# Rotary turns and head norms on pairs of tiles, the context's jobs emitted earlier, a longer pitch in the context's norms

## The chip, the core and the metric

The kernel runs on one core of a Trainium2 chip. The metric is the device time of one execution in microseconds; three runs of the kernel before gave 2795.01, 2799.68 and 2804.26 us, median 2799.68. Engines are PE (TensorE), DVE (VectorE), ACT (ScalarE), POOL (GpSimd) and SP, which issues the weight loads.

## What is computed

A sequence of 256 tokens with 1024 features goes through two blocks. The first has two layers: a pooling and gating mixer with a SwiGLU feed-forward, and a mixer of sparse attention (8 heads) and retention (4 heads) with another. The second has two layers, each feed-forward, attention, feed-forward, modulated by rows of an adaptive norm. It carries a context of 256 tokens beside the sequence:

```python
for i in range(2):
    m, mc = adaln(c, ada_w[i], ada_b[i]), adaln(c_ctx, ada_w[i], ada_b[i])
    h  = half_ffn(h,  m,  0, ...)              # the sequence
    hc = half_ffn(hc, mc, 0, ...)              # the context
    u, uc = modulated_norm(h, g[2], m, 3), modulated_norm(hc, g[2], mc, 3)
    y, yc = diff_attention(u, uc) if i == 0 else gqa_axial(u, uc)
    h = half_ffn(gated_residual(h, y, ...), m, 6, ...)
    if i == 0: hc = half_ffn(gated_residual(hc, yc, ...), mc, 6, ...)
```

Queries and keys get a rotary turn, `x * cos + swap(x) * sin`, where `swap` is a product with a fixed 128x128 matrix. Heads are normalised by their root mean square over 128 features (a head norm): after retention (4 tiles), after differential attention (8 tiles, sequence and context) and on queries and keys of the last attention (10 tiles of the sequence, 2 of the context).

## The kernel before

Activations lie with features on the partitions: a tile is 128 features by 256 tokens (`T`), so a 1024-wide activation is 8 tiles. Every dense product is done to full precision with three fp32r matmuls: a weight block of 128x2048 is loaded to `raw`, ACT copies it to `whi` (L208), DVE subtracts to `wlo` in two halves (L215, L228), and PE takes hi*hi, hi*lo and lo*hi (L249), 24 matmuls for each half block, 48 for a block.

Three generators produce work. `x_sequence` is the sequence (lane X), `c_sequence` the context (lane C), `modulation` the adaptive norm's rows (lane A). They yield `("D",)` before a block, `("d",)` between its two halves, and `("L", us)` where the next step should come no sooner than `us` of the planner's clock. X drives: at each of its D and d, `pace` (L1063) may take one or two steps of the others and adds 2.9 to the clock for a half block; at each of its L, `fill(us)` (L1049) advances the clock by 2.2 times `us` and takes dense steps of C (or A) as long as they are due. A step of C whose L is not over is not taken, and then `fill` leaves PE to X. Before each attention X calls `want("kv0")` or `want("kv1")`, which runs C to the end of its keys and values, whatever its L. The order thus made is the program order of every engine, and each engine's queue is served in that order.

- `turn` (L694) turns one tile: a 256-wide fp32 matmul with the swap matrix into a side bank (L698), then on DVE a product with sin from PSUM into `TMPX` (L700), a product with cos in place (L701) and a sum (L703). 41 tiles are turned: 15 in the sparse mixer, 16 in differential attention, 10 in the last. Where two or three banks are used in turn, the matmul of the third waits for L700 of the first.
- `tile_norm` (L721) works on one tile at a time: Square on ACT (L730), two column sums on PE (L736) with an L of 0.6 at every second tile, Sqrt (L741), reciprocal and scale (L744, L746); then per tile a diagonal (two 128-wide `tensor_scalar`, L753), its spreading with a ones matmul (L760), and the scaling (L766), with an L of 0.8 at every second tile; with `keep`, also a hi and lo part (L772, L778). X has two buffers for squares and diagonals, C one. 32 tiles are normalised.
- `norm` (L564) is the norm over 1024 features, with the residual. Its loop writes tile k of the next input in three steps over DVE, POOL and ACT (L607, L613, L656, L661, L670); in lane C it yields an L of 2.5 at every second turn, six in all. C goes through it five times.
- `after` (L279) holds back the job that empties a C bank (the gate's L428, the up product's L441, the down product's L492 with `put_out`, or an evacuation): it is emitted when C registers its next job, or by `settle` (L287) at the end of a part. Lane X emits its own at once.

## Time and profile before

| | |
|---|---|
| median of three runs | 2799.68 us |
| profiled execution | 2801.2 us, span 2799.5 us |
| PE busy | 2588.8 us (92%) |
| DVE busy | 1694.4 us (61%) |
| ACT busy | 1251.0 us (45%) |
| POOL busy | 132.2 us (5%) |
| mean granted TensorE clock | 0.959 |

The span runs from the first to the last instruction; the execution has 1.7 us around it. Busy time is the union of an engine's instructions. A wait is counted for the engine that sat idle, under the instruction that it waited with and the one that released it.

### The profile page before, as it was taken

The page shows a single profiled execution, that of the slowest core. Times are in us where ns is not written, and L with a number is a line of the kernel's source. Part 1 is how long each engine was busy: PE and PEld are TensorE (multiplying, and loading weights), DVE is VectorE, ACT ScalarE, POOL GpSimd, SP SyncE. Part 2 cuts the span into 40 slices and gives each one's busy share as a digit, 9 for nine tenths or more (in the row PEclk, how much of TensorE's full clock was granted, in tenths as well). Part 3 has the DMA queues.
Part 4 walks back from the last instruction along what each step waited for, and adds up shares of the span by engine and source line. Part 5 has one row for each costly group of instructions (what it writes and reads, how often), then busy time and mean ns, then how long its engine had stood idle before and what let it go on. Part 6 is the DMA issues. An engine that isn't in the chain of part 4 may idle for free.

```text
span 2799.5 us, 48887 instructions
## 1 busy us (share of the span) xinstructions
PE 2588.8 (92%) x20706; PEld 2461.9 (88%) x20706; DVE 1694.4 (61%) x2807; ACT 1251.0 (45%) x1698; POOL 132.2 (5%) x174
## 2 busy tenths in 40 slices
PE   6799998999998999999898999999999998987998
PEld 5699988888888899999797989999999998966998
DVE  5665564456666556466666757676566566555654
ACT  4533342344444344454444544454454454334443
POOL 0000000000012000000020000020000010000000
PEclk9899998899999999999899999999999999988999
DMA  6556655523445665544342334554545544444453
GB/s 231 196 187 248 242 181 193 211 104 108 166 163 199 222 247 185 192 153 155 103 144 83 121 124 168 179 174 165 182 168 181 177 166 144 165 147 170 151 178 124
DMA packets 68616, 475.80 MB, mean 170 GB/s; under 512 B 7984, under 2 KB 8496, under 8 KB 14768
## 3 DMA queue, kind: packets, MB, share of 16 engines
q1 hardware_dynamic: 66240, 468.74, 47.3%
q10 hardware_dynamic: 2160, 3.93, 0.5%
q8 instruction: 165, 2.70, 0.4%
q14 instruction: 51, 0.42, 0.0%
HBM read 471.60 MB, written 1.05 MB: 169 GB/s over the span
## 4 chain that ended last, share of the span: by engine, by line
PE 71%; DVE 11%; issue 7%; ACT 6%; DMA 4%; POOL 1%; ACTq 0%; DVEq 0%; POOLq 0%
PE bank L249 61%; ACT whi L208 4%; DVE wlo L228 2%; DMA raw<-w_main 2%; PE bank L994 2%; DVE wlo L215 1%; DMA raw<-w_down 1%; PE bank L876 1%; PE bank L814 1%; PE bank L1323 1%; PE bank L736 1%; DVE ARX L656 1%; DVE HNC_lo L670 1%; PE bank L760 1%; PE bank L864 1%
## 5 line engine op out<-in xcount | busy, mean ns | idle before, releaser
L249 PE MATMUL bank<-HNX_hi,whi 128*128 128x256 f32 x2968 | 866.4, 293 | 54.8 <-DVE wlo L228 30.9
L249 PE MATMUL bank<-HNX_hi,wlo 128*128 128x256 f32 x2968 | 851.8, 288 | 0.0
L208 ACT ACTIVATE whi<-raw 128x2048 fp32r<-128x2048 f32 (+1 forms) x378 | 705.6, 1867 | 306.2 <-PE bank L249 138.8
L249 PE MATMUL bank<-HNX_lo,whi 128*128 128x256 f32 x2968 | 838.5, 288 | 0.0
L215 DVE TENSOR_TENSOR wlo<-raw,whi 128x1024 fp32r<-128x1024 f32 (+1 forms) x378 | 454.3, 1202 | 605.5 <-ACT whi L208 604.8
L249 PEld LDWEIGHTS bank<-HNX_hi,whi 128*128 128x128 f32 x2968 | 585.9, 197 | 75.1 <-issue 46.1
L249 PEld LDWEIGHTS bank<-HNX_hi,wlo 128*128 128x128 f32 x2968 | 585.7, 197 | 0.0
L249 PEld LDWEIGHTS bank<-HNX_lo,whi 128*128 128x128 f32 x2968 | 577.8, 197 | 0.5
L228 DVE TENSOR_TENSOR wlo<-raw,whi 128x1024 fp32r<-128x1024 f32 (+1 forms) x378 | 453.1, 1199 | 0.0
L249 PE MATMUL bank<-HNC_hi,whi 128*128 128x256 f32 x1344 | 395.9, 295 | 20.2 <-DVE tmpc L428 9.5
L249 PE MATMUL bank<-HNC_lo,whi 128*128 128x256 f32 x1344 | 386.6, 288 | 0.0
L249 PE MATMUL bank<-HNC_hi,wlo 128*128 128x256 f32 x1344 | 386.4, 287 | 0.0
L249 PE MATMUL bank<-GX_hi,whi 128*128 128x256 f32 x1056 | 302.8, 287 | 3.0 <-DVE wlo L228 2.9
L249 PE MATMUL bank<-GX_lo,whi 128*128 128x256 f32 x1056 | 299.1, 283 | 0.0
L249 PE MATMUL bank<-GX_hi,wlo 128*128 128x256 f32 x1056 | 299.0, 283 | 0.0
L249 PEld LDWEIGHTS bank<-HNC_hi,whi 128*128 128x128 f32 x1344 | 264.4, 197 | 29.1 <-DVE tmpc L428 10.5
L249 PEld LDWEIGHTS bank<-HNC_lo,whi 128*128 128x128 f32 x1344 | 264.5, 197 | 0.5
L249 PEld LDWEIGHTS bank<-HNC_hi,wlo 128*128 128x128 f32 x1344 | 264.2, 197 | 0.0
L249 PEld LDWEIGHTS bank<-GX_hi,whi 128*128 128x128 f32 x1056 | 202.9, 192 | 8.9 <-DVE wlo L228 4.4
L249 PEld LDWEIGHTS bank<-GX_lo,whi 128*128 128x128 f32 x1056 | 202.9, 192 | 0.1
L249 PEld LDWEIGHTS bank<-GX_hi,wlo 128*128 128x128 f32 x1056 | 202.8, 192 | 0.0
L445 ACT ACTIVATE GX_hi<-tmpx 128x512 fp32r<-128x512 f32 x66 | 41.7, 632 | 262.5 <-DVE tmpx L441 262.5
(320 smaller groups left out, 3134.8 us busy)
## 6 DMA issues: line engine op xcount, KB each, us to landing
raw<-w_main SPq DMA_DIRECT2D x270, 1024.0 KB, 4.8
raw<-w_ada SPq DMA_DIRECT2D x72, 1024.0 KB, 4.8
raw<-w_down SPq DMA_DIRECT2D x72, 1024.0 KB, 4.9
raw<-w_down SPq DMA_DIRECT2D x36, 768.0 KB, 4.2
raw<-w_cmp SPq DMA_DIRECT2D x4, 1024.0 KB, 4.7
HX<-x_in SPq DMA_DIRECT2D x2, 512.0 KB, 6.2
HC<-ctx_in ACTq DMA_DIRECT2D x1, 1024.0 KB, 7.3
out<-HX SPq DMA_DIRECT2D x4, 256.0 KB, 2.1
```

What stands on the lines that cost most here:

```text
L208: NS.activation(WHI[q % HIS][:, 0:size], RAW[m % SLOTS][:, 0:size], ACT.Copy).then_inc(sems["w_hi"], 1)
L215: NV.tensor_tensor(WLO[m % SLOTS][:, 0:half], RAW[m % SLOTS][:, 0:half], WHI[q % HIS][:, 0:half].bitcast(fp32), SUB)
L228: NV.tensor_tensor(WLO[m % SLOTS][:, half:size], RAW[m % SLOTS][:, half:size], WHI[q % HIS][:, half:size].bitcast(fp32), SUB).then_inc(sem ...
L249: return NT.matmul(dst, (WHI[ordinal[n] % HIS], WLO[n % SLOTS])[w][:, k * 2 * P + col:k * 2 * P + col + P], x[xp][:, kx, :], start=start, ...
L445: NS.activation(g[0], S.TMP[p % 2][:, :], ACT.Copy).then_inc(hi.sem, 1)
L656: NV.scalar_tensor_tensor(S.Y[:, k, :], S.H[:, k, :], gain(k), S.wide_h[:, 0:T], MUL, MUL).then_inc(no.sem, 1)
L670: NV.scalar_tensor_tensor(S.HN[1][:, k, :], S.Y[:, k, :], shift(k), S.HN[0][:, k, :].bitcast(fp32), ADD, SUB)\
L736: mm = NT.matmul(sums[:, 2 * j + c:2 * j + c + 1], b[:, c * P:(c + 1) * P], ones[:, 0:1], start=True, stop=True)
L760: NT.matmul(bank[:, 0:T], ones, b[:, :], start=True, stop=True).then_inc(sp_.sem, 1)
L814: mm = NT.matmul(bank[:, c0 + c * T:c0 + (c + 1) * T], q[pr, :], k[pr, :], start=True, stop=True)
L864: mm = NT.transpose(turn_bank[:, c * P:(c + 1) * P], PB[w % 3][:, 0, c * P:(c + 1) * P], ident)
L994: mm = NT.matmul(bank[32 * g:32 * g + 32, 0:T], CCOL[:, k, 6 - 2 * r:38 - 2 * r], RAW[n % SLOTS][:, k * T:(k + 1) * T], start=r == 0 and k ...
```

## The change

- `turn` takes a pair of tiles (one stays alone): one 512-wide matmul and three 512-wide DVE operations. 21 calls in place of 41.
- `tile_norm` takes pairs: one 512-wide Square, four column sums, one diagonal as a `tensor_tensor` of 512 with two broadcast inputs, one 512-wide spreading matmul, one scaling (two after retention, whose gains differ). An L of 0.8 stands ahead of every pair's sums and one of 1.0 ahead of every pair's spreading. The product with 1.0 is left out. X's buffers are `TMPX[1]` and the joined squares buffer, C's is `TMPC[1]`. 16 pairs in place of 32 tiles.
- `catch_up` at the head of `pace` and `fill` emits C's held job as soon as a further block of any lane has been taken.
- The L in the loop of C's `norm` is 6.0 in place of 2.5.

```diff
-        SQX, SQC = [sb(f"sqx{s}", [P, T])[:, :] for s in range(2)], [sb("sqc", [P, T])[:, :]]
+        SQ2, SQC = sb("sqx", [P, 2 * T]), [sb("sqc", [P, T])[:, :]]
+        SQX = [SQ2[:, s * T:(s + 1) * T] for s in range(2)]
...
                 last, jobs[S.tag] = jobs.get(S.tag), job
+                behind[0] = len(taken)
                 if last:
                     last()
+
+            def catch_up():
+
+                if "c" in jobs and len(taken) > behind[0]:
+                    settle(C)
...
                     if t == "c" and j % 2 == 0:
-                        yield ("L", 2.5)
+                        yield ("L", 6.0)
                     if t == "x" and j == 4:
                         yield ("L", 4.0)
...
-            def turn(tile, rot, cos, sin, bank, j, *ready):
+            def turn(tiles, rot, cos, sin, bank, j, *ready):
 
                 turned, part, straight, done_ = up("pe_step"), up("dve_step"), up("dve_step"), up("dve_step")
+                n = tiles.shape[1]
+                swapped, kept = (x[:, 0:n * T].rearrange("p (a b) -> p a b", a=n) for x in (bank, TMPX[j % 2]))
                 if on(pe, free.get(bank.name), *ready):
-                    NT.matmul(bank[:, 0:T], rot, tile, start=True, stop=True).then_inc(turned.sem, 1)
+                    NT.matmul(swapped, rot, tiles, start=True, stop=True).then_inc(turned.sem, 1)
                 if on(dve, turned):
-                    NV.tensor_tensor(TMPX[j % 2][:, 0:T], bank[:, 0:T], sin, MUL).then_inc(part.sem, 1)
-                    NV.tensor_tensor(tile, tile, cos, MUL).then_inc(straight.sem, 1)
+                    NV.tensor_tensor(kept, swapped, sin.unsqueeze(1).to_broadcast([P, n, T]), MUL).then_inc(part.sem, 1)
+                    NV.tensor_tensor(tiles, tiles, cos.unsqueeze(1).to_broadcast([P, n, T]), MUL).then_inc(straight.sem, 1)
                     dve.wait_ge(*straight)
-                    NV.tensor_tensor(tile, tile, TMPX[j % 2][:, 0:T], ADD).then_inc(done_.sem, 1)
+                    NV.tensor_tensor(tiles, tiles, kept, ADD).then_inc(done_.sem, 1)
                 free[bank.name] = part
                 return done_
...
 
-            def tile_norm(S, items, gain, factor, ready, eps, sums, banks, keep=False):
-
-
-                n, last = len(items), {}
-                buf = S.TMP[0][:, 0:2 * n]
-                for j, src in enumerate(items):
+            def tile_norm(S, pairs, gain, factor, ready, eps, sums, banks, keep=False, alike=True):
+
+
+                n, last = len(pairs), {}
+                buf = S.TMP[0][:, 0:4 * n]
+                wide = [S.TMP[1][:, :]] if S.lag else [S.TMP[1][:, :], SQ2[:, :]]
+                for j, src in enumerate(pairs):
                     sq = up("act_step")
-                    b = S.SQ[j % len(S.SQ)]
-                    if on(act, last.get(j - len(S.SQ)), *ready):
-                        NS.activation(b[:, :], src, ACT.Square).then_inc(sq.sem, 1)
-                    if j % 2:
-                        yield ("L", 0.6)
+                    b = wide[j % len(wide)]
+                    if on(act, last.get(j - len(wide)), *ready):
+                        NS.activation(b.rearrange("p (a q) -> p a q", a=2), src, ACT.Square).then_inc(sq.sem, 1)
+                    yield ("L", 0.8)
                     total = up("pe_step")
                     if on(pe, sq, free.get(sums.name) if j == 0 else None):
-                        for c in range(2):
-                            mm = NT.matmul(sums[:, 2 * j + c:2 * j + c + 1], b[:, c * P:(c + 1) * P], ones[:, 0:1], start=True, stop=True)
+                        for c in range(4):
+                            mm = NT.matmul(sums[:, 4 * j + c:4 * j + c + 1], b[:, c * P:(c + 1) * P], ones[:, 0:1], start=True, stop=True)
                         mm.then_inc(total.sem, 1)
                     last[j] = total
-                root, inv, fac = up("act_step"), up("dve_step"), up("dve_step")
+                root, inv = up("act_step"), up("dve_step")
+                fac = inv if factor is None else up("dve_step")
                 if on(act, total):
-                    NS.activation(buf, sums[:, 0:2 * n], ACT.Sqrt, bias=eps, scale=1.0 / P).then_inc(root.sem, 1)
+                    NS.activation(buf, sums[:, 0:4 * n], ACT.Sqrt, bias=eps, scale=1.0 / P).then_inc(root.sem, 1)
                 free[sums.name] = root
                 if on(dve, root):
                     NV.reciprocal(buf, buf).then_inc(inv.sem, 1)
                     dve.wait_ge(*inv)
-                    NV.tensor_scalar(buf, buf, 1.0 if factor is None else factor, None, MUL).then_inc(fac.sem, 1)
+                    if factor is not None:
+                        NV.tensor_scalar(buf, buf, factor, None, MUL).then_inc(fac.sem, 1)
                 spreads, his, los, marks = {}, [], [], []
 
                 def diagonal(j):
-                    b, bank, diag = S.SQ[j % len(S.SQ)], banks[j % len(banks)], up("dve_step")
-                    if on(dve, fac, spreads.get(j - len(S.SQ)), total):
-                        for c in range(2):
-                            op = NV.tensor_scalar(b[:, c * P:(c + 1) * P], ident, buf[:, 2 * j + c:2 * j + c + 1], None, MUL)
-                        op.then_inc(diag.sem, 1)
+                    b, diag = wide[j % len(wide)], up("dve_step")
+                    if on(dve, fac, spreads.get(j - len(wide)), total):
+                        NV.tensor_tensor(b.rearrange("p (c q) -> p c q", c=4), ident.unsqueeze(1).to_broadcast([P, 4, P]),
+                                         buf[:, 4 * j:4 * j + 4].unsqueeze(2).to_broadcast([P, 4, P]), MUL).then_inc(diag.sem, 1)
                     return diag
 
                 def spread(j, diag):
-                    b, bank, sp_ = S.SQ[j % len(S.SQ)], banks[j % len(banks)], up("pe_step")
+                    bank, sp_ = banks[j % len(banks)], up("pe_step")
                     if on(pe, diag, free.get(bank.name)):
-                        NT.matmul(bank[:, 0:T], ones, b[:, :], start=True, stop=True).then_inc(sp_.sem, 1)
+                        NT.matmul(bank[:, :], ones, wide[j % len(wide)], start=True, stop=True).then_inc(sp_.sem, 1)
                     spreads[j] = sp_
 
-                def scale_tile(j):
+                def scale_pair(j):
                     bank, sc = banks[j % len(banks)], up("dve_step")
                     if on(dve, spreads[j]):
-                        NV.scalar_tensor_tensor(items[j], items[j], gain(j), bank[:, 0:T], MUL, MUL).then_inc(sc.sem, 1)
+                        if alike:
+                            NV.scalar_tensor_tensor(pairs[j], pairs[j], gain(2 * j), bank[:, :].rearrange("p (a q) -> p a q", a=2), MUL, MUL)\
+                                .then_inc(sc.sem, 1)
+                        else:
+                            for m in range(2):
+                                op = NV.scalar_tensor_tensor(pairs[j][:, m, :], pairs[j][:, m, :], gain(2 * j + m), bank[:, m * T:(m + 1) * T], MUL, MUL)
+                            op.then_inc(sc.sem, 1)
                     free[bank.name] = sc
                     marks.append(sc)
                     if keep:
                         hi = up(f"{S.tag}_hn_hi")
                         if on(act, sc):
-                            NS.activation(S.HN[0][:, j, :], items[j], ACT.Copy).then_inc(hi.sem, 1)
+                            NS.activation(S.HN[0][:, 2 * j:2 * j + 2, :], pairs[j], ACT.Copy).then_inc(hi.sem, 1)
                         his.append(hi)
 
                 def keep_low(j):
                     lo = up(f"{S.tag}_hn_lo")
                     if on(dve, his[j]):
-                        NV.tensor_tensor(S.HN[1][:, j, :], items[j], S.HN[0][:, j, :].bitcast(fp32), SUB).then_inc(lo.sem, 1)
+                        NV.tensor_tensor(S.HN[1][:, 2 * j:2 * j + 2, :], pairs[j], S.HN[0][:, 2 * j:2 * j + 2, :].bitcast(fp32), SUB).then_inc(lo.sem, 1)
...
                     los.append(lo)
                 diag = diagonal(0)
                 for j in range(n + 1):
                     if j < n:
-                        if j % 2 == 0:
-                            yield ("L", 0.8)
+                        yield ("L", 1.0)
                         spread(j, diag)
-                        if len(S.SQ) > 1 and j + 1 < n:
+                        if len(wide) > 1 and j + 1 < n:
                             diag = diagonal(j + 1)
-                        scale_tile(j)
-                        if len(S.SQ) == 1 and j + 1 < n:
+                        scale_pair(j)
+                        if len(wide) == 1 and j + 1 < n:
                             diag = diagonal(j + 1)
...
             def fill(us, passing=0.0):
 
+                catch_up()
                 if ahead["c"] == "W":
...
             def pace(kind):
 
+                catch_up()
                 if ahead["c"] == "W":
                     step("c")
...
-                for j, t in enumerate((4, 6, 8)):
-                    roped = turn(Z[:, t, :], *ROT, side[j], j, z_kv[-1])
+                for j, t in enumerate((4, 8)):
+                    roped = turn(Z[:, t:t + 3 - 2 * j:2, :], *ROT, side[j], j, z_kv[-1])
...
+                todo = [(z0[-1], t) for t in (8, 10)]
                 for b, at in [(7, 14), (8, 16), (9, 18), (10, 20), (11, 22), (0, 0), (1, 2), (2, 4), (3, 6)]:
-                    for j, (m, t) in enumerate(todo[:2]):
-                        roped = turn(Z[:, t, :], *ROT, side[j], j, m)
-                    todo = todo[2:]
+                    for m, t in todo[:1]:
+                        roped = turn(Z[:, t:t + 2, :], *ROT, side[t // 2 % 2], t // 2, m)
+                    todo = todo[1:]
...
-                nrm = yield from tile_norm(X, [RO[:, h, :] for h in range(4)], lambda h: vec("gn_g", h, 1), None, [cen, g1], vec("eps5"), BANK[4], BANK[2:4])
+                nrm = yield from tile_norm(X, [RO[:, h:h + 2, :] for h in (0, 2)], lambda h: vec("gn_g", h, 1), None, [cen, g1], vec("eps5"), BANK[4], BANK[2:4], alike=False)
...
-                normed = [0, 1, *range(4, 12)]
-                nqk = yield from tile_norm(X, [Z[:, t, :] for t in normed], lambda j: vec("k_norm" if j < 2 else "q_norm"), None, [z[-1], vt],
+                normed = [0, 4, 6, 8, 10]
+                nqk = yield from tile_norm(X, [Z[:, t:t + 2, :] for t in normed], lambda j: vec("k_norm" if j < 2 else "q_norm"), None, [z[-1], vt],
...
-                kn = yield from tile_norm(C, [KC[:, g, :] for g in range(2)], lambda j: vec("k_norm"), None, [zk[-1]], vec("eps6"), BANK[7], BANK[6:7])
+                kn = yield from tile_norm(C, [KC[:, 0:2, :]], lambda j: vec("k_norm"), None, [zk[-1]], vec("eps6"), BANK[7], BANK[6:7])
```

The other callers of `turn` and `tile_norm` change in the same way.

## Rows read from the trace of the kernel before

**Rows 1.** The page: busy time, share and instructions of each engine; engines' shares of the chain.
```profile
PE 2588.8 (92%) x20706; PEld 2461.9 (88%) x20706; DVE 1694.4 (61%) x2807; ACT 1251.0 (45%) x1698; POOL 132.2 (5%) x174
...
PE 71%; DVE 11%; issue 7%; ACT 6%; DMA 4%; POOL 1%; ACTq 0%; DVEq 0%; POOLq 0%
```

**Rows 2.** PE's waits, whole span: in total us, times, longest us.
```profile
PE bank L249 <- DVE wlo L228: 35.5, 17, 7.7
...
PE bank L760 <- DVE sqc L753: 9.7, 5, 3.0
PE bank L249 <- DVE tmpc L428: 9.5, 5, 3.2
...
PE bank L760 <- DVE sqx L753: 7.8, 8, 1.5
...
PE bank L249 <- DVE tmpc L441: 5.4, 4, 2.8
...
PE bank L736 <- ACT sqc L730: 4.5, 5, 1.5
...
PE bank L698 <- DVE tmpx L700: 4.1, 9, 0.7
...
PE bank L736 <- ACT sqx L730: 3.3, 3, 1.2
PE bank L249 <- DVE ARC L492: 2.4, 1, 2.4
```

**Rows 3.** Groups by line: busy us, mean ns of one, idle before, releaser.
```profile
L428 DVE SCALAR_TENSOR_TENSOR tmpx<-tmpx,bank 128x512 f32<-128x512 f32 x66 | 45.3, 686 | 53.1 <-ACT tmpx L426 52.9
...
L700 DVE TENSOR_TENSOR tmpx<-bank,ARX 128x256 f32<-128x256 f32 x41 | 17.2, 420 | 24.5 <-PE bank L698 24.5
...
L766 DVE SCALAR_TENSOR_TENSOR ARX<-ARX,VEC,bank 128x256 f32<-128x256 f32 x22 | 10.5, 478 | 3.1 <-PE bank L760 3.0
...
L1312 DVE TENSOR_TENSOR ARX<-ARX 64x480 f32<-64x480 f32 x4 | 3.9, 968 | 4.2 <-PE bank L1323 4.1
...
L1517 PE MATMUL bank<-ARX,VEC 128*128 128x512 f32 x4 | 2.0, 590 | 0.0
```

**Rows 4.** The chain in order of time, 1372 to 1406 us: start, us, what.
```profile
1377.42 2.98 PE bank L249 x24
...
1383.67 0.40 DVE sqc L753 x2
...
1384.12 1.22 PE bank L760 x2
1385.34 3.83 PE bank L249 x24
```

**Rows 5.** Timeline, 1378 and 908 us on: start, us, instruction, idle before and releaser.
```profile
1380.12 0.74 PEld L698 LDWEIGHTS bank<-ARX,VEC 128*128 128x128 f32 x4
...
910.86 1.89 ACT L208 ACTIVATE whi<-raw 128x2048 fp32r<-128x2048 f32 x1
...
915.50 1.22 DVE L228 TENSOR_TENSOR wlo<-raw,whi 128x1024 fp32r<-128x1024 f32 x1
...
916.87 0.55 PE L249 MATMUL bank<-HNX_hi,whi 128*128 128x256 f32 x1 [6.74 <-DVE wlo L228]
```

**Rows 6.** Busy time in four stretches: us, then PE, PEld, DVE, ACT, POOL, clock, DMA share, GB/s.
```profile
136.00:172.00 36.00, 31.16 (x216) 29.79 (x217) 25.75 (x54) 14.42 (x20) 5.75 (x8) 0.81 0.35 123
...
1487.00:1511.00 24.00, 12.54 (x68) 9.91 (x69) 19.56 (x47) 13.17 (x29) 5.75 (x8) 0.79 0.05 18
1511.00:1618.00 107.00, 106.27 (x866) 99.84 (x864) 74.10 (x130) 58.13 (x105) 0.00 (x0) 1.00 0.34 119
...
2449.00:2485.00 36.00, 27.05 (x111) 18.12 (x111) 20.17 (x62) 6.70 (x14) 0.00 (x0) 0.76 0.15 49
```

**Rows 7.** Instructions of L661 and L760: duration ns min/median/max, first and last start.
```profile
L661 ACT ACTIVATE HNC_hi<-ARC,MOD x40: 494/508/513, 117.8 to 2334.1; 128x256 fp32r<-128x256 f32 x40
...
L760 PE MATMUL bank<-sqc,VEC x20: 377/379/797, 1381.1 to 2371.6; 128*128 128x256 f32 x20
```

More of the change, by code:

```diff
@@ L163, in program @@
             NV, NS, NT, NG = nc.vector, nc.scalar, nc.tensor, nc.gpsimd
-            taken, split_at, opened, jobs = [], [0, 0, 0], [None], {}
+            taken, split_at, opened, jobs, behind = [], [0, 0, 0], [None], {}, [0]
             free, passed, gains_known = {}, set(), {}
@@ L1337, in x_sequence @@
                 blk = blocks_of(1, hid)
-                for t in range(4):
-                    roped = turn(Z[:, t, :], *ROT, side[t % 2], t, z_q[-1])
+                for t in range(0, 4, 2):
+                    roped = turn(Z[:, t:t + 2, :], *ROT, side[t // 2], t // 2, z_q[-1])
                 z_v = yield from linear(X, "od_in", [(9, 18), (10, 20)], Z)
@@ L1356, in x_sequence @@
                 z_rk = yield from linear(X, "od_in", [(7, 14)], Z)
-                for j, t in enumerate(range(10, 14)):
-                    roped = turn(Z[:, t, :], *ROT, side[j % 2], j, z_rq[-1])
+                for j, t in enumerate((10, 12)):
+                    roped = turn(Z[:, t:t + 2, :], *ROT, side[j], j, z_rq[-1])
                 turned, th = up("pe_step"), up("act_step")
@@ L1375, in x_sequence @@
                 z_rg = yield from linear(X, "od_in", [(11, 22)], Z)
-                for j, t in enumerate(range(14, 18)):
-                    roped = turn(Z[:, t, :], *ROT, side[j % 2], j, z_rk[-1])
+                for j, t in enumerate((14, 16)):
+                    roped = turn(Z[:, t:t + 2, :], *ROT, side[j], j, z_rk[-1])
                 z_rg = yield from linear(X, "od_in", [(12, 24)], Z)
@@ L1555, in x_sequence @@
                     dve.wait_ge(*in_tab)
-                todo = [(z0[-1], t) for t in range(8, 12)]
+                todo = [(z0[-1], t) for t in (8, 10)]
                 for b, at in [(7, 14), (8, 16), (9, 18), (10, 20), (11, 22), (0, 0), (1, 2), (2, 4), (3, 6)]:
-                    for j, (m, t) in enumerate(todo[:2]):
-                        roped = turn(Z[:, t, :], *ROT, side[j], j, m)
-                    todo = todo[2:]
+                    for m, t in todo[:1]:
+                        roped = turn(Z[:, t:t + 2, :], *ROT, side[t // 2 % 2], t // 2, m)
+                    todo = todo[1:]
                     z = yield from linear(X, "da_in", [(b, at)], Z)
                     if b == 7:
-                        todo += [(z1[-1], t) for t in (12, 13)] + [(z[-1], t) for t in (14, 15)]
+                        todo += [(z1[-1], 12), (z[-1], 14)]
                     elif b < 4:
-                        todo += [(z[-1], t) for t in (at, at + 1)]
+                        todo.append((z[-1], at))
                     if b == 11:
@@ L1568, in x_sequence @@
                 vt = None
-                for j, (m, t) in enumerate(todo):
-                    roped = turn(Z[:, t, :], *ROT, side[j % 2], j, m)
+                for m, t in todo:
+                    roped = turn(Z[:, t:t + 2, :], *ROT, side[t // 2 % 2], t // 2, m)
                 vt = by_token([Z[:, 16 + h, c * P:(c + 1) * P] for c in range(2) for h in range(8)], VTX, side, z_v)
@@ L1580, in x_sequence @@
                 passed.add("x_da")
-                x = yield from tile_norm(X, [YX[:, h, :] for h in range(8)], lambda h: vec("subln"), 1.0 - LAMBDA_INIT, [o], vec("eps6"), BANK[4], BANK[2:4], True)
+                x = yield from tile_norm(X, [YX[:, h:h + 2, :] for h in range(0, 8, 2)], lambda h: vec("subln"), 1.0 - LAMBDA_INIT, [o], vec("eps6"), BANK[4], BANK[2:4], True)
                 free["x", "gain"] = need(0, 5)
@@ L1612, in x_sequence @@
                 for j, t in enumerate(normed):
-                    roped = turn(Z[:, t, :], *ROT, side[j % 3], j, nqk)
+                    roped = turn(Z[:, t:t + 2, :], *ROT, side[j % 3], j, nqk)
                 want("kv1")
@@ L1685, in c_sequence @@
                 o = yield from attend_context(units, 0.125, PB, PT, LAM, [vt, l5, zq[-1]])
-                x = yield from tile_norm(C, [YC[:, h, :] for h in range(8)], lambda h: vec("subln"), 1.0 - LAMBDA_INIT, [o], vec("eps6"), BANK[7], BANK[6:7], True)
+                x = yield from tile_norm(C, [YC[:, h:h + 2, :] for h in range(0, 8, 2)], lambda h: vec("subln"), 1.0 - LAMBDA_INIT, [o], vec("eps6"), BANK[7], BANK[6:7], True)
                 free["c", "gain"] = yield from await_rows(0, 5)
```

## The prediction

> **What bounds the kernel now.** First the page: PE is busy 92% of the span, and 71% of the chain that ended last is PE, 11% DVE [rows 1]. So the time is PE's work plus the 210.7 us in which it idles (2799.5 less 2588.8), and an edit pays as far as it shortens one of the two. DVE at 61% is no bound on average; locally it is. The second view is the list of PE's waits [rows 2]: the largest, 35.5 us, is for a block's `wlo`, that is for DVE (and ACT before it) being late with a weight block. Then come the head norms: 9.7 and 7.8 us for diagonals (C's and X's), 4.5 and 3.3 for squares. Waits for a C bank that its job hasn't emptied are 9.5 (L428), 5.4 (L441) and 2.4 us (L492), and turns wait 4.1 us for one another's bank. The third view is the busy time by stretch [rows 6], which tells where C's blocks cover X's gaps, and what is left bare.
>
> **Head norms and turns, PE.** Both spreads of two tiles stand in one step, so the second waits until DVE has scaled the first and made the next diagonal. At 1384.12 this ends in two passes of 1.22 us, and the 24 matmuls behind it take 3.83 us where the ones ahead took 2.98 [rows 4]: the clock had fallen. In the change each spread has its own L, so a half block of 2.98 us stands between two. That covers 0.69 us of diagonal (the 686 ns of a 512-wide PSUM operation stands for it [rows 3]) and 0.75 of scaling (478 ns plus 256 columns at the slope of L700 to L428, 420 to 686, so 744). Of the 17.5 us of waits for diagonals I take off 14.5; 3 stay, the first diagonal of each norm and the last attention, where no C block is left. Of 7.8 for squares I take off 4.8: the sums that stood right behind their Square now have an L between, but the first of each norm may still come late. Of 4.1 for side banks 3.6 go: no group in the sparse mixer has a third turn any more. The waits of turns for L392's evacuation stay, since a pair waits for the same one. Warm clock regained: 0.85 us behind the wait in rows 4, three to four such places, 3 us.
>
> Matmul width: the second 256 columns of a 512-wide matmul cost 590-379 = 211 ns a pass (L1517 against the warm L760 [rows 3, 7]), two passes. Two tiles apart take four passes, paced by four weight loads in 0.74 us (at 1380.12 [rows 5]), so 0.19 each; a pair takes two of 0.21 and its loads behind another's passes, 0.55. So 0.2 us a pair, of 20 turn pairs and 16 norm pairs less the ten in the last attention where DVE bounds: 26 x 0.2 = 5.2 us.
>
> The last attention's head norm and turns lie bare: 2449 to 2485, PE at clock 0.76 [rows 6]. The turns there run at DVE's pace, three operations; each pair saves three fixed parts of 420-266 = 154 ns, 5 x 0.46 = 2.3 us, less 0.7 for a longer first matmul and its last pair. Spreads take two scalings and four diagonals (0.2 us each, 0.40 for two [rows 4]) in a pair of tiles, 1.7 us with the waits 2.2; in pairs 1.3 to 1.5: 5 x 0.8 = 4 us, of which about 2 are already in the waits. Sum 3.5. The column sums stay as many, and they set the pace of the squares.
>
> Sum of this part: 14.5+4.8+3.6+3+5.2+3.5 = 34.6; I take 33, since part of the freed time meets the next wait, `wlo`. From below: if DVE only hands the wait on, half, 17. From above 40.
>
> The price that the trace doesn't show is the diagonal with an input that stands still along the row (one scalar for 128 columns). Bounds: 0.69 us as for any 512-wide operation, and 0.97 for 480 elements with a still input and a strided one (L1312 [rows 3]). I take 0.69, since only one of L1312's inputs is like it and the strides there are long; at 1.0 it would be 16 x 0.3 = 5 us of DVE, behind half blocks mostly, 2 us of the end.
>
> The skill speaks against this edit: the Trainium skill, VectorE: DVE Perf Modes, "The perf-mode tier table (the rule you actually need)", gives fp32 `tensor_scalar` two elements a cycle and `tensor_tensor` one. By it the pair's 512 columns would stream 0.27 us longer, 4.3 us over 16 pairs. The rows have the four old operations at 0.8 us together, so the saved fixed parts pay for it, and no term of the sum changes.
>
> **C's jobs emitted earlier.** C's bank waits sum to 17.3 us (9.5+5.4+2.4) [rows 2], 10 places. A job held from a block long past, with X's blocks since, is emitted with `catch_up` behind the next block; then the bank is free long before C returns. Where two C blocks follow each other within one `fill`, nothing changes. I take 9 of 17.3. The last four down products of C's feed-forward emit three `put_out` in a row, and the longest wait for `wlo` (7.7 us) is of that kind; spread by one block each, it loses 3 us. What is moved is ACT's and DVE's work alone (no DMA, SP's queue isn't passed; POOL gets its sums a block sooner). The job now stands in front of X's second `wlo` half at places; it waits for a C block that PE has ended or is ending, so it holds up DVE for a microsecond or so, and the half is needed two blocks later: 0 to +5 us, taken as 0. Sum -12, from -20 to +5.
>
> **Longer pitch in C's norms.** Five norms (40 hi tiles, 117.8 to 2334.1 [rows 7]), six steps each: 6 x 3.5 = 21 planner units more, about 21 us at 2.9 a half block of 2.98. A step puts some 2.6 us on DVE, an estimate: 19.56 us busy in 1487 to 1511 [rows 6], less 3 units at about 3.1, over four steps. A block's `wlo` takes 2 x 1.22 [rows 5] beside it. At one step a half block DVE has more work than PE: at 910.86 `whi` starts late behind C's tiles on ACT, `wlo` ends at 916.7, and PE has idled 6.74 us [rows 5]. With the pitch of 6.0 a step falls on two to three half blocks, and DVE fits. Gain: 8 us at 916 with its cold clock, and of the same kind 4, 3 and 2 at three others, an estimate from the rest of the 35.5 us: -17.
>
> Against it stands the cover. X's own `fill`s can only take dense steps of C when C isn't in an L. (a) 136 to 172: C's first norm ends just ahead of X's norm, and two C blocks fill it. Now C is still in its own norm; the two blocks (11.9 us) come later, in X's full stretches, and X's gap saves perhaps 6 of them: +6. (b) 1487 to 1511: C's norm of six steps lies over the first units of X's attention, PE 12.5 of 24 us [rows 6]. A filled unit takes 107/16, so 6.7 us at most, and PE is full then [rows 6]. At 6.0 a step takes two `fill`s (3.0+4.0 planner units), so the six last about four units longer. Each bare unit takes 4.2 to 5.9 us with no C block of 5.96 in it, which costs 3 to 4: 4 x 3.5 = +14 with the relief of what stalls there now. (c) C's end comes later, so its last norm meets X's norm: +2. Sum -17+22 = +5, from -15 to +25.
>
> **Sum.** -33-12+5 = -40 on the profiled execution's 2801.2 us gives 2761. The order of the blocks changes from the first norm on, and new waits of the weight split can't be read from rows of another order: an allowance of +4 for them, one longish wait of rows 2. Forecast 2765 us; the profiled execution is 1.5 us above the median of the runs shown, so nothing is to be shifted.
>
> **Rivals.**
> 1. The waits are handed on: DVE is as busy as before near the norms, and what goes from rows 2 at L760 and L736 comes back at `wlo`. For it: 35.5 us are waits for DVE already, and C's head norm stands where DVE is fullest. Against it: pairs also take work off DVE (turns 41 x 3 x 0.42 = 52 us against 21 x 3 x 0.69 = 43). Then -17-5+5: 2784 us.
> 2. The cover lost is nothing: C's later blocks fill X's norm at the last attention, as bare as 2449 to 2485. Then (a) to (c) cancel: -33-12-17 gives 2739 us.
> 3. The pitch costs more than all gives: C ends too late. Its last head norm is at 2371.6 [rows 7], and X wants kv1 at about 2484 [rows 6]: 112 us. Three norms at +21 make 63, and the four blocks left over in the attention come at one for one of X's, 4 x 11.9 = 48: 111. From there on `want` runs C's rest bare: norm chain, two blocks, a head norm, 35 us. Against it: the planner's clock runs 2.2 times in X's `fill`s, which carries C's L steps along. It decides from the point where C ends later than X's turns. Then -33-12+5, +35 for the bare rest and +20 as the waits are handed on as in rival 1: 2816 us, slower.
> 4. It does nothing that can be told: gains of 20 and losses of 20, 2800 us.
>
> **Chances.** The measurement tells about 0.3%, 8.4 us. Forecast (2752 to 2778) 0.50; rival 1 (2779 to 2792) 0.20; rival 2 (2735 to 2751) 0.14; no difference 0.09; rival 3 0.07. Faster 0.84, same 0.09, slower 0.07. Range 2738 to 2794: it leaves out rival 3, rival 4 and the far end of rival 2.
>
> **What would show it.** Right: waits at L760 and L736 under 7 us together (25.3 now); L698 for L700 near nothing; C's waits for L428 and L441 at half; no 6.7 us gap in C's second norm; the bare stretch around 2449 shorter by 3 to 4; PE less busy by 5; C's hi tiles of the third norm spread over some 40 us. Wrong: `wlo` waits above 35 us; a diagonal above 0.8 us; C's kv1 head norm behind X's turns.

## The result and the profile after

The kernel after takes 2736.55 us (median of 4 runs, 2734.23 to 2740.13), the kernel before, measured beside it, 2799.51: ratio 0.9776, 95% interval 0.9756 to 0.9796. That is 63 us less, where 35 were forecast; 2736.55 is 1.5 us below the lower end of the range. The direction was right, the size was not.

The page after, the two lines that answer to [rows 1]:

```profile
PE 2561.5 (94%) x20634; PEld 2428.9 (89%) x20634; DVE 1677.2 (61%) x2674; ACT 1241.1 (45%) x1668; POOL 127.7 (5%) x174
...
PE 76%; DVE 11%; ACT 5%; issue 3%; DMA 3%; POOL 1%; ACTq 0%; DVEq 0%; POOLq 0%
```

The span fell from 2799.5 to 2733.6 us. PE's idle time fell from 210.7 to 172.1, by 38.6 us, and its busy time by 27.3. The prediction counted mostly waits, and took only some 8 us off PE's own work (5.2 for the width, 3 for the clock).

PE's waits after, whole span (in total us, times, longest), against [rows 2]:

```profile
PE bank L250 <- DVE wlo L229: 25.5, 18, 6.0
PE bank L250 <- ACT HNX_hi L668: 14.9, 12, 5.3
PE bank L879 <- DVE ARX L843: 12.9, 7, 3.1
PE bank L250 <- ACT HNX_hi L666: 12.6, 5, 5.6
...
PE bank L829 <- DVE KC L777: 4.9, 1, 4.9
...
PE bank L250 <- DVE tmpc L435: 2.9, 1, 2.9
...
PE bank L745 <- ACT tmpx L740: 2.3, 2, 1.5
...
PE bank L250 <- DVE tmpc L448: 2.1, 2, 1.1
...
PE bank L770 <- DVE tmpc L763: 0.7, 1, 0.7
...
PE bank L707 <- DVE tmpx L709: 0.2, 1, 0.2
```

(L760 is L770 now, L736 L745, L698 L707, L428 L435, L441 L448.) Diagonals cost 0.7 us in place of 17.5, squares 2.5 in place of 7.8, the side banks 0.2 in place of 4.1, C's banks (L435, L448) 5.0 in place of 14.9, `wlo` 25.5 in place of 35.5. What grew stands in the second to fourth line: the waits for the hi tiles of X's own norms (L668 from 4.0 us, L666 from 8.5), and those for L843, the DVE step that combines the two softmax parts in X's differential attention (from 0.8). There PE waited before for ACT's exponentials instead, 9.7 us in two waits against 2.3 in one now.

The groups by line with shapes apart, for the price that was not to be seen before (busy us, mean ns of one, idle before):

```profile
L763 DVE TENSOR_TENSOR tmpx<-VEC,tmpx 128x512 f32<-128x512 f32 x6 | 4.1, 688 | 0.2
...
L777 DVE SCALAR_TENSOR_TENSOR ARX<-ARX,VEC,bank 128x512 f32<-128x512 f32 x9 | 6.7, 744 | 8.7 <-PE bank L770 8.7
...
L709 DVE TENSOR_TENSOR tmpx<-bank,ARX 128x512 f32<-128x512 f32 x20 | 13.8, 688 | 23.6 <-PE bank L707 23.6
...
L712 DVE TENSOR_TENSOR ARX<-ARX,tmpx 128x512 f32<-128x512 f32 x20 | 13.9, 693 | 0.7
```

The broadcast diagonal takes 0.69 us, the value taken and not the 0.97 of L1312 in [rows 3]; the scaling 744 ns is what was worked out. The four `tensor_scalar` of a pair before (L753) kept DVE busy for 0.95 us, 15.2 us in all over the 16 pairs; the 16 new diagonals take 10.9.

### The profile page after: what moved, and what is told of

Same layout as the page of the kernel before. It is cut to its first block, busy times and chain, and to the rows that moved or that the text cites. A ratio compares the mean times of both kernels' runs of the same rounds, so it can differ in the third digit from the quotient of the medians.

```text
span 2733.6 us, 48496 instructions
## 1 busy us (share of the span) xinstructions
PE 2561.5 (94%) x20634; PEld 2428.9 (89%) x20634; DVE 1677.2 (61%) x2674; ACT 1241.1 (45%) x1668; POOL 127.7 (5%) x174
## 4 chain that ended last, share of the span: by engine, by line
PE 76%; DVE 11%; ACT 5%; issue 3%; DMA 3%; POOL 1%; ACTq 0%; DVEq 0%; POOLq 0%
PE bank L250 66%; ACT whi L209 3%; DMA raw<-w_main 2%; DVE wlo L229 2%; PE bank L1009 2%; DVE wlo L216 1%; DMA raw<-w_down 1%; PE bank L891 1%; PE bank L829 1%; DVE ARX L663 1%; PE bank L1340 1%; DVE tmpx L614 1%; PE bank L707 1%; DVE HNX_lo L677 1%; PE bank L879 1%
## 5 line engine op out<-in xcount | busy, mean ns | idle before, releaser
L250 PE MATMUL bank<-HNX_hi,whi 128*128 128x256 f32 x2968 | 865.8, 293 | 58.9 <-DVE wlo L229 21.1
L250 PEld LDWEIGHTS bank<-HNC_hi,whi 128*128 128x128 f32 x1344 | 259.2, 193 | 17.3 <-issue 6.9
```

The costliest lines, as they stand in the source:

```text
L250: return NT.matmul(dst, (WHI[ordinal[n] % HIS], WLO[n % SLOTS])[w][:, k * 2 * P + col:k * 2 * P + col + P], x[xp][:, kx, :], start=start, ...
```

## The experiments

Ratios are to the kernel before on the same chip, with a 95% interval; a difference in us is taken from the ratio or the medians, which agree within 3 us. "Idle" is the span less PE's busy time of the profiled execution (210.7 us before).

**The three parts alone.** First the pairs without the two others.

```diff
-                        yield ("L", 6.0)
+                        yield ("L", 2.5)
...
             def fill(us, passing=0.0):
 
-                catch_up()
...
             def pace(kind):
 
-                catch_up()
```

> The change's pairs alone (turns and head norms), C's jobs held as before, pitch 2.5. The changed kernel gained 63 us where 35 were forecast, so a term was too small. Theory 1 (the pairs' term was right, 33 us, and another was wrong): 2767 us, ratio 0.988. Theory 2 (the pairs carry the surplus as well, since every DVE operation saved comes back as PE time): 2745 us or less, ratio 0.980. In both the waits at the spreading matmul and the sums fall from 25.3 to under 7 us.

Measured 2763.53 us, 0.9871 (0.9857 to 0.9886): -36. Idle fell by 22.9, busy by 14.5:

```profile
PE 2574.3 (93%) x20634; PEld 2441.6 (88%) x20634; DVE 1680.8 (61%) x2674; ACT 1246.5 (45%) x1674; POOL 132.4 (5%) x174
```

The waits for `wlo` stay (33.6 us), so nothing was handed on to them; C's banks (L435, L448, L499) came to 21.1 us in place of 17.3, so some 4 us were handed on there.

The earlier emission alone, on the kernel before:

```diff
             def fill(us, passing=0.0):
 
+                catch_up()
...
             def pace(kind):
 
+                catch_up()
```

> The early emission of C's jobs alone, single tiles, pitch 2.5. Theory 1 (as forecast): 12 us, ratio 0.996. Theory 2 (its term was the small one: bank waits 17.3 us go nearly whole, and the wait for the weight split that three jobs in a row cause goes as well, with the clock): 25 us or more, ratio 0.991. A rival: it stands in front of X's second half of the weight split and gives nothing, ratio 1.0.

Measured 2781.36 us, 0.9938 (0.9923 to 0.9953): -18. Its page and its waits:

```profile
PE 2582.5 (93%) x20706; PEld 2455.3 (88%) x20706; DVE 1690.2 (61%) x2807; ACT 1253.2 (45%) x1698; POOL 129.6 (5%) x174
```

```profile
PE bank L249 <- DVE wlo L228: 38.5, 21, 6.7
...
PE bank L249 <- DVE tmpc L434: 6.0, 2, 3.0
...
PE bank L249 <- DVE ARC L498: 1.3, 1, 1.3
...
PE bank L249 <- DVE tmpc L447: 1.0, 1, 1.0
```

C's bank waits are 8.3 us in place of 17.3: the 9 that were taken. `wlo` gave nothing (38.5 for 35.5, though its longest went from 7.7 to 6.7). Idle fell by 13.7 and busy by 6.3, with the same 20,706 matmuls.

The longer pitch alone:

```diff
-                        yield ("L", 2.5)
+                        yield ("L", 6.0)
```

> The pitch of 6.0 in the loop of C's norm alone. Theory 1 (as forecast): 17 us gained where the steps crowd DVE and ACT, 22 lost for blocks of C that no longer fill X's gaps, together 5 us slower, ratio 1.002. Theory 2 (the loss was overstated, since fill runs the planner's clock 2.2 times as fast and the norm in the attention is hardly longer): 10 to 17 us faster, ratio 0.995.

Measured 2786.63 us, 0.9962 (0.9947 to 0.9976): -11, where +5 was forecast. Here the prediction failed.

Emission and pitch together:

> Early emission and pitch 6.0, single tiles. If the parts add up, its gain is the sum of the two alone. If they work on the same stall (DVE and ACT crowded where C's feed-forward ends and its norm begins), it is less than the sum by some 5 us; theory 1 has 7 us (ratio 0.9975), theory 2 has 35 (0.9875).

Measured 2773.04 us, 0.9907 (0.989 to 0.9924): -26, against 18+11 = 29. The three parts add within the noise: 36+18+11 = 65, against 63. No cost of a new order of blocks, beyond what each part carries, is to be seen.

**The pitch, norm by norm.** A counter makes the pitch 6.0 in chosen norms of C only; the numbers in the list change from kernel to kernel.

```diff
+                nth[0] += t == "c"
...
-                        yield ("L", 2.5)
+                        yield ("L", 6.0 if nth[0] in (1,) else 2.5)
```

> The kernel before, with the pitch of 6.0 in C's first norm alone (the other four keep 2.5). The prediction's term (a): C's first norm ends after X's, the two C blocks that filled X's norm (11.9 us) stand in X's full stretches instead: +6 us, 2806. Rival (the cover lost is nothing, because C's half blocks of its own norm lie in X's gap instead, or C's blocks find another gap): within 2 us of 2799.5. The longer pitch as a whole measured about 11 to 13 us of gain; if that came from norm 1, 2790.

Measured 2790.54 us, 0.9983 (0.9973 to 0.9992): -5, not +6. X's norm lay as bare as forecast. The windows of it (us, then PE, PEld, DVE, ACT, POOL, clock, DMA share, GB/s):

```profile
133.00:163.00 30.00, 17.16 (x97) 13.94 (x98) 21.97 (x52) 13.03 (x20) 5.72 (x8) 0.66 0.30 114
```

PE works 17 of 30 us at a clock of 0.66. X's first gate comes at 162.9 us in place of 170.1: 7.2 us earlier with two C blocks (11.9 us) fewer, so 4.7 were lost, near the 6 of term (a).

Where do the two blocks come instead? X's six feed-forwards cut the span into seven stretches that hold the same X work in every run (lane A's differs by up to 24 matmuls), and C's blocks in each can be counted. Of the matmuls that read the hi tiles of C's norms (two of the three products of a block), the third stretch, from X's second feed-forward to its third, has in the kernel before, and then with 6.0 in the first norm (us; PE; clock; DMA share, GB/s):

```profile
806.20:1092.70 286.50, 30.34 (x160) 0.98 0.59 212
```

```profile
788.70:1084.70 296.00, 42.28 (x224) 0.97 0.59 212
```

64 more are 96 matmuls with the low parts, that is the two blocks (its down products, which read other tiles, are as many in both). They stand in X's full stretch, as the prediction said, and lengthen it by some 9.6 us. So term (a) as told comes to 9.6-7.2, +2.4. What makes the run faster lies between: the second stretch, from the first to the second feed-forward, is 10.3 us shorter with the same 28 blocks of C. Its idle time is 27.2 us in place of 34.6. One wait that is gone is the fourth of PE's from 290 to 806 us before,

```profile
PE bank L1008 <- ACT rows L1003: 4.3, 1, 4.3
```

and waits for C's banks are 8.1 in place of 10.9. No block was spent on it that the kernel before didn't spend there too; C only runs two blocks further behind. Why that order idles less was not tried.

> The kernel before, with the pitch of 6.0 in C's third norm alone. The prediction's term (b): four more units of X's differential attention stay bare at 3.5 us each, +14 us, 2813. Rival: the attention's bare units are paid back, since a C block that isn't spent beside the first units covers later ones, so the term is nothing: 2797 to 2801. A third way: the norm doesn't spread over the attention's units at all (the planner's clock runs 2.2 times there, so that a step of 6.0 takes not much more than one call), and the relief of DVE makes it faster by 3 to 5, 2795.

Measured 2802.79 us, 1.0017 (1.0008 to 1.0027): +5, a third of the +14. Two waits grew over the whole span, `wlo` (35.5 before) and the combining step of X's attention (0.8 before, while its exponentials went from 9.7 to 2.3):

```profile
PE bank L249 <- DVE wlo L228: 41.9, 18, 7.7
PE bank L865 <- DVE ARX L829: 14.4, 7, 3.9
```

> The kernel before, with the pitch of 6.0 in C's second, fourth and fifth norm. The prediction's gain of 17 us (8 at 916, the rest at the others): 2783 to 2785. If the gain is DVE's relief but smaller, as the whole pitch measured, 2788 to 2790. Theory that the pitch gains nothing by itself but shifts the order: no telling, 2795 to 2803.

Measured 2781.53 us, 0.995 (0.9934 to 0.9967): -14, against the 17 forecast. The wait of 6.74 us at 916 in [rows 5] is gone; from 880 to 940 us PE waits 2.3 us in all for `wlo`.

```profile
PE bank L249 <- DVE wlo L228: 28.4, 18, 7.7
...
PE bank L249 <- DVE tmpc L428: 6.4, 4, 3.1
```

The three add: -5+5-14 = -14, against -11 together. The stretches of the profiled executions, in us with C's blocks in brackets, show where it comes from. "Before" is the kernel before, then 6.0 in the named norms alone; then three versions in the changed order, which are the subject of the next part. Stretches that a run leaves alone differ by up to some 4 us between executions.

| stretch, up to the first gate of X's | before | 1st | 3rd | 2nd, 4th, 5th | changed order, 2.5 in all | after | after, 2.5 in 3rd |
|---|---|---|---|---|---|---|---|
| 1st feed-forward | 170.1 (2) | 162.9 (0) | 172.0 (2) | 168.4 (2) | 173.7 (2) | 163.3 (0) | 161.0 (0) |
| 2nd | 636.2 (28) | 625.8 (28) | 635.9 (28) | 636.1 (28) | 619.5 (28) | 610.5 (28) | 613.5 (28) |
| 3rd | 286.4 (8) | 296.0 (10) | 288.3 (8) | 281.2 (8) | 282.7 (8) | 290.0 (10) | 290.1 (10) |
| 4th, behind differential attention | 654.2 (36) | 651.3 (36) | 630.3 (31) | 652.6 (36) | 632.5 (36) | 607.9 (31) | 631.1 (36) |
| 5th | 364.6 (27) | 364.6 (27) | 360.8 (26) | 322.2 (21) | 361.7 (27) | 325.7 (21) | 320.0 (21) |
| 6th, behind the last attention | 494.2 (16) | 494.1 (16) | 520.2 (22) | 522.9 (22) | 484.1 (16) | 542.5 (27) | 514.7 (22) |

The rest behind the 6th gate takes 194 us in all of them. A C block's own work is 5.96 us. With 6.0 in the second, fourth and fifth norm, the second norm gives 5 us (286.4 to 281.2, with the same blocks). The larger part is six blocks that leave the fifth stretch, which gets 42.4 us shorter, and come in the sixth, which gets only 28.7 longer: their work is 35.8 us, so 7 were gained where they left and 7 where they came. With 6.0 in the third norm, five blocks fewer make X's attention stretch 23.9 us shorter (29.8 would be no loss), and six more the sixth 26.0 longer. By the profiled executions these stretches together lose nothing; the medians of ten runs say +5.

**The pitch in the changed order.** The kernel after with 2.5 in the first and third norm, then in the third alone (the diff), then with 9.0 in the four others, with 2.5 in all five, and once more as it is.

```diff
-                        yield ("L", 6.0)
+                        yield ("L", 2.5 if nth[0] in (3,) else 6.0)
```

> The kernel after, with the pitch of 2.5 again in C's first and third norm. If the prediction's terms (a) and (b) hold in this order too, it beats the kernel after by up to 20 us, 2717 to 2730. If the longer pitch pays or costs nothing at these two, it is as fast as the kernel after or slower: 2735 to 2745.

Measured 2733.73 us, 0.9778 (0.9764 to 0.9793): as the kernel after.

> The kernel after, with the pitch of 2.5 again in C's third norm alone. In the order of before the longer pitch cost 5 us in the third norm and gained 5 in the first. If both are so here too: 2731 to 2732, and 2 us less than with 2.5 in the first and third. If the order matters more than the pitch, anything from 2728 to 2742.

Measured 2724.46 us, 0.9725 (0.971 to 0.974): 12 us below the kernel after (0.9776, 0.9756 to 0.9796; by the ratios 14); the intervals don't meet. This is the fastest version of the case.

> The kernel after, with the pitch of 2.5 in C's third norm and 9.0 instead of 6.0 in the other four. If DVE still stalls PE in these norms at 6.0, it gains 2 to 5 us on the kernel with 6.0 there, 2728; if they are relieved already, C's norms only end later, and X's stretches behind them go bare: 2735 to 2745.

Measured 2728.15 us, 0.9738 (0.9721 to 0.9754): no gain over 6.0 in these four; the intervals of the two overlap.

> The kernel after with the old pitch of 2.5 in all five of C's norms (so pairs and earlier jobs alone). If the parts add up as they did on the kernel before, 36+18 = 54: 2746, and the longer pitch is worth 10 here. If the third norm's +12 to +14 is of the changed order and the other four give more here (the kernel with 2.5 in the first and third was 9 us slower than the one with 2.5 in the third alone): again near 2744 to 2750. If the pitch is worth nothing in the changed order: 2737.

Measured 2751.02 us, 0.9826 (0.981 to 0.9842).

> The kernel after once more, on the chip of this call, to stand beside the others: 2736 to 2737.

Measured 2738.99 us, 0.9781 (0.9766 to 0.9795), as the first time.

So in the changed order the pitch is worth 12 us (2751.0 to 2739.0). By ratios, on 2800 us: norms 2, 4 and 5 give 0.9826-0.9778, 13 us; the first 0.9778-0.9725, 15 (each interval is 4 us wide to a side, and the profiled spans say 5: 2729.6 and 2724.2); the third costs 15 (spans: 9 and 13). What the third norm does is seen in two windows of the kernel after, X's attention with C's norm over it and its filled rest:

```profile
1444.00:1469.00 25.00, 15.30 (x92) 11.60 (x91) 23.52 (x55) 13.98 (x35) 5.75 (x8) 0.80 0.00 1
1469.00:1543.00 74.00, 71.58 (x584) 66.48 (x580) 54.35 (x101) 40.28 (x75) 0.00 (x0) 1.00 0.30 102
```

and in the same of the kernel with 2.5 in the third:

```profile
1445.00:1462.00 17.00, 6.85 (x36) 4.41 (x32) 16.01 (x38) 9.49 (x21) 4.63 (x7) 0.62 0.00 1
1462.00:1563.00 101.00, 100.64 (x806) 94.70 (x807) 71.42 (x129) 54.55 (x97) 0.00 (x0) 0.98 0.34 116
```

The bare part is 8 us longer, though it idles about as much (9.7 and 10.2 us); the filled part is 27 us shorter. The five C blocks that go missing there come back in the sixth stretch, all of them ahead of X's last attention. Matmuls that read C's hi tiles from the end of X's fifth gate phase to there, in the kernel after and then with 2.5 in the third:

```profile
2208.00:2416.00 208.00, 44.62 (x224) 0.95 0.44 154
```

```profile
2223.00:2407.00 184.00, 11.84 (x64) 0.94 0.44 148
```

By the table the longer pitch in the third norm makes the fourth stretch 23.2 us shorter here and the sixth 27.8 longer, and the fifth 5.7 longer with the same 21 blocks. Those 10 us are the price in the profiled executions. The first norm repeats what it did alone. From the run with 2.5 in the first and third to the one with 2.5 in the third, the first stretch goes from 172.3 to 161.0 us, the third from 276.9 to 290.1 with the two blocks, and the second from 619.4 to 613.5 with the same blocks.

**Inside the pairs.** Turns alone on pairs, head norms as before:

```diff
-                for j, t in enumerate(range(10, 14)):
-                    roped = turn(Z[:, t, :], *ROT, side[j % 2], j, z_rq[-1])
+                for j, t in enumerate((10, 12)):
+                    roped = turn(Z[:, t:t + 2, :], *ROT, side[j], j, z_rq[-1])
```

> The kernel before with the rotary turns alone on pairs of tiles (head norms as before). By the prediction's own terms: side banks 3.6, matmul width 0.2 us for some 15 pairs that PE bounds, 3.0, and 1.6 in the bare last attention, together 8: 2791. Rival: a pair of turns is one longer DVE operation in front of a weight half, so what PE saves comes back at wlo: 2797 to 2800. If the turns carry half of the 36 us that the pairs measured, 2781.

Measured 2794.19 us, 0.9977 (0.9968 to 0.9987): -6 to -8, near the 8 of the turns' terms. The side banks' waits went from 4.1 to 0.2 us. So the head norms carry some 29.

The spreads one by one, each with an L of its own, tiles as before:

```diff
-                        if j % 2 == 0:
-                            yield ("L", 0.8)
+                        yield ("L", 0.8)
                         spread(j, diag)
```

> The kernel before, with only the placement of its head norms' spreads changed: one spread of one tile in each step (an L before each), instead of two in every second. The squares stay as they are. If the half block between two spreads is what the pairs gain in the head norms, waits for diagonals go from 17.5 to some 3 us and the warm clock comes back: 2799.5-14.5-3 = 2782. If it is the width (half as many passes, diagonals and scalings), this gives little: 2793 to 2800. The doubled steps also move C's blocks, 5 us either way.

Measured 2789.31 us, 0.9959 (0.9943 to 0.9975): -12 of the 29. The waits for diagonals fell from 17.5 to 4.3 us:

```profile
PE bank L760 <- DVE sqc L753: 2.7, 4, 0.8
...
PE bank L760 <- DVE sqx L753: 1.6, 2, 1.4
```

PE is busy for 2585.5 us (2588.8 before), so this removes waits and little else. Idle fell by 7.5 us only, not by the 13.2 of the diagonals: X's attention (the combining step, 0.8 to 7.6) and the hi tiles of X's norms (L659, 8.5 to 12.0) wait longer. The other 17 us of the head norms are a difference, not a run. In them are the squares, whose waits stay at 8.4 us here and are 1.7 with pairs, and the width: with pairs alone PE's busy time at the spreads went from 25.4 us (64 passes; 23.2 in this run) to 19.3 (32), at the sums from 21.6 to 18.0 (128 either way), and at the turns from 25.6 to 22.2.

**Where the emission pays.** The earlier emission in `fill` alone, without the call in `pace`:

```diff
             def pace(kind):
 
-                catch_up()
```

> The kernel before with the earlier emission only at X's planned gaps (in fill), not behind X's dense blocks (not in pace). If C's jobs wait mostly behind X's dense blocks, where the C block comes alone, little is left of the 18 us: 2795. If it is the gaps: 2783. The prediction took 9 us off bank waits and 3 off wlo; the whole edit took 9 off bank waits, and the rest of its 18 us came as PE busy less and other idle time.

Measured 2790.40 us, 0.9964 (0.9953 to 0.9976): -10 of the 18. Waits for C's banks are 10.6 us, between the 17.3 before and the 8.3 of the whole edit. X's gaps give over half, and the difference is what its dense blocks add.

## Why the prediction came out 28 us short

**Head norms and turns, -33.** Measured -36: right, and the waits went as named: 3.2 us at diagonals and squares together (under 7 foretold, 25.3 before), the turns' side banks at nothing. Inside the term the sizes were shifted: with pairs alone these waits fell from 29.4 to 4.4 us, by 25 where 22.9 were taken, but half blocks between spreads alone brought 12 us and not 17.5, and PE's own time at the three steps fell by more than the 5.2 of "26 x 0.2". PE was forecast less busy by 5 through the width and by 3 through a warm clock; it is by 14.5. The clock's part was right, 3.1 us at the blocks' matmuls (2238.1 to 2235.0); spreads, sums and turns take 13 us less, of which 2 came with the spreads' placement alone. Together that is 16, of which 14.5 show in PE's busy time. The bare last attention, from its first column sums to X's scores, takes 27.4 us with pairs alone and 32.6 before: 5.2, where 3.5 and the 2 counted in the waits were taken.

**C's jobs, -12.** Measured -18. The 9 us of bank waits were right to a tenth. The 3 us of `wlo` didn't come (38.5 for 35.5), but idle time fell by 13.7 all the same. The step that was missing is PE's work: 6.3 us less of it for the same matmuls. Of the 17,688 matmuls of the blocks alone (L249), busy time in the kernel before, with the earlier emission, with the longer pitch, and after (us; PE; PEld; clock; DMA share, GB/s):

```profile
0.00:2900.00 2900.00, 2238.12 (x17688) 2189.76 (x17688) 0.96 0.47 164
```

```profile
0.00:2900.00 2900.00, 2233.15 (x17688) 2184.82 (x17688) 0.96 0.46 164
```

```profile
0.00:2900.00 2900.00, 2228.57 (x17688) 2181.55 (x17688) 0.96 0.46 164
```

```profile
0.00:2900.00 2900.00, 2225.14 (x17688) 2173.98 (x17688) 0.97 0.46 164
```

The work is the same, its time falls by 5.0, 9.6 and 13.0 us. The clock's mean over the span went from 0.959 to 0.967 at the same time. The traces tell the granted clock at the moment each of these matmuls starts (for some 30 they tell none): 499 stand at the lower level (0.5, 1.2 GHz) in the kernel before, 443 with the earlier emission, 421 with the longer pitch, 340 in the kernel after. One there adds 227 ns to PE's busy time in the kernels before and after, one at 2.4 GHz 123 and 124. So it is the clock that gives the 13 us: 159 matmuls fewer at the lower level, at 0.10 us each, would be 16, and those at the full level take 3 more in sum. The prediction gave the clock 3 us, at "three to four such places", in the head norms only, and none for the waits that the two other parts remove.

**Longer pitch, +5.** Measured -11 alone and -12 in the changed order. This is the step that failed. The size of its gain was right (-17 forecast, -14 measured for norms 2, 4 and 5), though not its make-up: in the profiled execution the second norm gave 5 us where 8 were taken, and of 14 in the fifth and sixth stretch 7 came from six blocks that found gaps in the sixth. Its costs, +22, were charged as if cover that is lost in one place were lost for good, and as if nothing else moved:

- (a), +6, came out as -5. In the profiled execution the two blocks do "come later, in X's full stretches", and cost 9.6 us there against the 7.2 that X's norm gets shorter: +2.4. What the term put at nothing is the stretch between: it is 10.3 us shorter with the same blocks (5.9 in the changed order). Its cause stays open.
- (b), +14, came out as +5 alone and as 12 to 15 in the changed order. C's hi tiles of the third norm lie over 17 us (the row below; 12.5 with 2.5) and not over 40, so the bare part is longer by 8 us and not by four units. The failed step is "4 x 3.5": five C blocks fewer lost 5.9 us of cover in X's attention stretch, 1.2 a block, and the blocks cost less than their work in the sixth stretch (26.0 us for six). In the changed order it is dearer for two reasons that the table shows and doesn't explain: five blocks cost 27.8 there, and the fifth stretch is 5.7 longer.

```profile
L668 ACT ACTIVATE HNC_hi<-ARC,MOD x8: 498/508/511, 1452.8 to 1469.6; 128x256 fp32r<-128x256 f32 x8
```

- (c), +2, was not tried apart; norm 5 was in the group that gained, and its sixth stretch took six blocks (35.8 us) for 28.7.

**Allowance, +4.** It was for waits in a new order of blocks, and none is left over: the parts add to 65, the whole is 63.

The difference of 28 us is then: pitch 16 or 17, emission 6, pairs 3, allowance 4 (30; the parts add to 2 more than the whole).

**The rivals.** Rival 1, waits handed on, is refuted: with pairs alone `wlo` is 33.6 for 35.5, and the 4 us more at C's banks are far from half. Rival 2, the cover lost is nothing, came nearest (2739), and it had 0.14. Its mechanism is seen: two of C's late blocks stand in X's last head norm, which PE fills to 31.9 of 37 us at a clock of 0.91, where [rows 6] have 27 of 36 at 0.76:

```profile
2376.00:2413.00 37.00, 31.88 (x186) 24.61 (x186) 15.13 (x25) 7.61 (x13) 0.00 (x0) 0.91 0.27 90
```

That its sum came so near is luck in part: it has -33-12-17 where -36-18-11 were measured, and the gain between the first two feed-forwards is not in it. Rival 3's point was reached: X's last attention waits 4.9 us for C's kv1 head norm, whose scaling starts on DVE at 2415.1 us, right behind the last operation of X's turns. With 2.5 in the third norm the same place waits as long for X's own turn, so reaching it cost less than a microsecond:

```profile
PE bank L830 <- DVE ARX L713: 5.0, 1, 5.0
```

Of the signs of error, `wlo` above 35 and a diagonal above 0.8 us did not come in the kernel after (`wlo` was 38.5 with the earlier emission alone); the third, kv1's head norm behind X's turns, did come, by one DVE operation of 0.74 us. Of the signs of being right, C's hi tiles over some 40 us did not.

## What to carry to other kernels

When a wait of TensorE goes, price what the clock gives back too: here 38.6 us of idle time went with 27 us of busy time, some 13 of them on unchanged work. Where a second lane's blocks fill the first one's gaps, cut the span into stretches of equal work, count the blocks in each, and follow a moved block to where it lands: two cost 9.6 us of their 11.9 in a full stretch, six cost 26 to 29 of their 35.8 in one that had gaps left. Then set such a pitch place by place: the same 6.0 gained at four norms and cost 12 us at the one that lies over the attention.

## What the runs showed of the hardware

A DVE `tensor_tensor` of 128x512 in fp32 takes 684 to 688 ns (means of the three groups) with an input that stands still along 128 columns (L763), as plain ones do from SBUF (L712, 693) and one from PSUM with an input repeated for two tiles (L709, 688): the broadcast was free here. The clock's price shows in equal matmuls: one of the blocks' adds 123 ns at the full level and 227 at the lower one, and with 159 fewer at the lower one the 17,688 took 13 us less.
